# Where the mixer turns of a hybrid RG-LRU / attention block split three of their weight tiles

## The reference, cut to what matters

```python
xn = modulate(x, norm_mix_g, mx[0], mx[1]);  cn = modulate(ctx, norm_mix_g, mc[0], mc[1])
xr, kx, vx, gx, qx, mrx, mnx = jnp.split(xn @ w_in, IN_SPLITS, axis=-1)   # 7 column blocks of 1024
cr, kc, vc = jnp.split(cn @ w_in[:, :CTX_KV_COLS], [D_RNN, D_RNN + D_ATT], axis=-1)
h_x, _ = rglru_bidirectional(dwconv(xr), dwconv(cr), ...)                 # input branch
y_rnn = h_x * gelu(gx)
y_na = neighborhood_attention(rope_2d(qx), qx, rope_2d(kx), vx, kc, vc, na_rpb)
merged = sigmoid(mrx) * (y_rnn @ w_rnn_out) + sigmoid(mnx) * (y_na @ w_na_out)
x = x + mx[2] * (merged @ w_out)
x = x + mx[5] * conv_ffn(modulate(x, norm_ffn_g, mx[3], mx[4]), ...)
```

## Time and profile before

| | |
|---|---|
| median of three runs | 2131.47 us (2130.02 to 2133.41) |
| profiled execution, own time | 2128.76 us |
| its span | 2126.9 us |
| granted TensorE clock, mean | 0.997 of full speed |
| PE busy, share of the span | 2051.1 us, 96% |
| VectorE busy | 1628.0 us, 77% |
| ScalarE busy | 1072.5 us, 50% |
| GpSimd busy | 492.8 us, 23% |

### The profile page before, as it was taken

How to read it: one execution, slowest core, us unless ns; L and a number is a source line. 1 busy time by engine, 2 the same in 40 slices (tenths; PEclk the granted TensorE clock), 3 DMA queues, 4 the chain that set the end, 5 groups by cost and what they waited for, 6 DMA issues and landing times.

```text
span 2126.9 us, 28320 instructions
## 1 busy us (share of the span) xinstructions
PE 2051.1 (96%) x10618; PEld 1739.8 (82%) x10618; DVE 1628.0 (77%) x2809; ACT 1072.5 (50%) x1631; POOL 492.8 (23%) x377
## 2 busy tenths in 40 slices
PE   5999999999999999999998899999999999999999
PEld 1878888988988889888887788887788888887887
DVE  6688598596885985859859866767998888877766
ACT  3466666665676657656666621002444334434332
POOL 0031130222212212212123010000124442115550
PEclk9999999999999999999999999999999999999999
DMA  8421211112012120120111385453347764239663
GB/s 328 112 64 41 62 51 47 47 53 70 30 41 72 40 73 20 53 70 30 43 50 69 106 310 193 144 188 131 89 134 197 183 176 118 94 122 335 226 205 126
DMA packets 105576, 241.65 MB, mean 114 GB/s; under 512 B 27264, under 2 KB 32768, under 8 KB 104960
## 3 DMA queue, kind: packets, MB, share of 16 engines
q1 hardware_dynamic: 74304, 191.08, 26.4%
q0 software_dynamic: 14592, 44.05, 8.0%
q10 hardware_dynamic: 16544, 4.72, 1.0%
HBM read 203.11 MB, written 63.96 MB: 126 GB/s over the span
## 4 chain that ended last, share of the span: by engine, by line
PE 77%; DVE 13%; ACT 4%; issue 2%; ACTq 0%; DVEq 0%
PE banks L47 14%; PE banks L49 14%; PE banks L48 14%; PE banks L991 4%; PE banks L862 4%; PE banks L864 4%; PE banks L863 4%; PE banks L895 3%; PE banks L2269 3%; PE banks L2270 3%; PE banks L2271 3%; DVE probT_low L1494 2%; PE banks L953 2%; DVE prob L1486 2%; PE banks L935 1%
## 5 line engine op out<-in xcount | busy, mean ns | idle before, releaser
L47 PE MATMUL banks<-qh,xnh 128*128 128x384 f32 (+1 forms) x640 | 223.3, 349 | 0.3 <-PEq L216 0.3
L862 PE MATMUL banks<-xnh,wh 128*128 128x512 f32 (+1 forms) x536 | 211.3, 394 | 3.2 <-ACT stage L1097 2.9
L49 PE MATMUL banks<-qh,xnl 128*128 128x384 f32 (+1 forms) x640 | 207.7, 325 | 0.0
L48 PE MATMUL banks<-ql,xnh 128*128 128x384 f32 (+1 forms) x640 | 207.6, 324 | 0.0
L864 PE MATMUL banks<-xnh,wl 128*128 128x512 f32 (+1 forms) x536 | 204.5, 381 | 0.0
L863 PE MATMUL banks<-xnl,wh 128*128 128x512 f32 (+1 forms) x536 | 204.1, 381 | 0.0
L1494 DVE TENSOR_TENSOR probT_low<-banks,probT_high 128x512 fp32r<-128x512 f32 (+2 forms) x256 | 138.9, 583 | 56.2 <-ACT probT_high L1165 55.2
L1165 ACT CAST probT_high<-banks 128x512 fp32r<-128x512 f32 (+2 forms) x256 | 117.0, 510 | 60.3 <-PE banks L953 51.4
L47 PE MATMUL banks<-yh,wh 128*128 128x512 f32 x372 | 145.0, 390 | 0.9 <-DVE wl L2471 0.9
L48 PE MATMUL banks<-yl,wh 128*128 128x512 f32 x372 | 145.0, 390 | 0.0
L49 PE MATMUL banks<-yh,wl 128*128 128x512 f32 x372 | 144.9, 390 | 0.0
(11 more groups left out here) (396 smaller groups left out, 6015.9 us busy)
## 6 DMA issues: line engine op xcount, KB each, us to landing
raw<-w_ff SPq DMA_DIRECT2D x33, 512.0 KB, 5.7
down_d<-w_down POOLq DMA_DIRECT2D x66, 256.0 KB, 6.9
raw<-w_fm SPq DMA_DIRECT2D x32, 512.0 KB, 6.7
extras<-h_d SPq DMA_DIRECT2D x55, 256.0 KB, 3.9
raw<-w_qkv SPq DMA_DIRECT2D x24, 512.0 KB, 3.9
raw<-w_mix SPq DMA_DIRECT2D x24, 512.0 KB, 4.8
h_d<-conv_d SPq DMA_DIRECT2D x21, 512.0 KB, 3.2
raw<-w_modT SPq DMA_DIRECT2D x16, 512.0 KB, 4.6
```

The lines of the kernel that those rows point to most:

```text
L47: pe.matmul(out, w_hi(k), x_hi(k), start=(k == 0), stop=False)
L48: pe.matmul(out, w_hi(k), x_lo(k), start=False, stop=False)
L49: last = pe.matmul(out, w_lo(k), x_hi(k), start=False, stop=(k == chunks - 1))
L862: pe.matmul(out, fh[:, s, k, :], xnh[:, k, c0:c1], start=(k == 0), stop=False)
```

## The change

- Middle turns: `split_hi`/`split_low` of XR and MR go behind query tile 1 and its gates. 
- Turns 0 to 6: `split_hi(MN)` goes in front of `branch(F_MR)`, behind the last conv input (the input branch's last matmul); `split_low(MN)` goes in front of `maxima(0)`.
- Last turn: `split_hi(MN)`/`split_low(MN)` go behind query tile 1, so that MN is now split before MR; `LAST_ORDER` and one wait of SP follow. `split_hi(MR)`/`split_low(MR)` stay.
- Turn 0 keeps its splits of XR and MR where they were.

```diff
--- before.py
+++ after.py
@@ -587,7 +587,7 @@
         SLOT = {XR: 0, G: 1, MR: 1, MN: 0}
         RAW = {Q0: 0, Q1: 1, Q2: 2, XR: 0, MR: 1, MN: 2, G: 0}
         ORDER = {Q0: 0, Q1: 1, Q2: 2, XR: 3, MR: 4, MN: 5, G: 6}
-        LAST_ORDER = {Q0: 0, Q1: 1, Q2: 2, MR: 3, MN: 4}
+        LAST_ORDER = {Q0: 0, Q1: 1, Q2: 2, MN: 3, MR: 4}
 
         def split_count(u, i, last=False):
             return i * UNITS + 2 + (LAST_ORDER if last else ORDER)[u] + 1
@@ -747,7 +747,7 @@
                     store_stage(smr_d, i, 1, 1)
                     store_stage(smn_d, i, 0, 2)
                     sp.wait_ge(yr_out, PAIRS * 16)
-                    sp.wait_ge(w_lo, split_count(MN, i, True))
+                    sp.wait_ge(w_lo, split_count(MR, i, True))
                     for k in range(2):
                         load_y(k)
                     sp.dma_start(raw[:, 2, :], w_mix[0]).then_inc(mix_in, 16)
@@ -1222,6 +1222,8 @@
                     for s in range(1, 4):
                         q_evac(i, s)
                         gate_pieces(i, *GATES_LAST[s])
+                        if s == 1:
+                            split_hi(MN, raw_count(MN, i))
                     decays(i, 0)
                     q_evac(i, 4)
                     root(i, 0)
@@ -1233,6 +1235,9 @@
                     for s in range(3):
                         q_evac(i, s, first)
                         gate_pieces(i, *GATES_AFTER[s])
+                        if s == 1:
+                            split_hi(XR, raw_count(XR, i))
+                            split_hi(MR, raw_count(MR, i))
                     decays(i, 0)
                     q_evac(i, 3)
                     q_evac(i, 4)
@@ -1240,11 +1245,10 @@
                     gate_pieces(i, *GATES_AFTER[4])
                     q_evac(i, 5)
                     gate_pieces(i, *GATES_AFTER[5])
-                if not last:
+                if first:
                     split_hi(XR, raw_count(XR, i))
-                split_hi(MR, raw_count(MR, i))
-                if last:
-                    split_hi(MN, raw_count(MN, i))
+                if first or last:
+                    split_hi(MR, raw_count(MR, i))
                 q_evac(i, 6)
                 gate_pieces(i, *(GATES_FIRST if first else GATES_AFTER)[6])
                 if first:
@@ -1522,6 +1526,11 @@
                     outputs(i - 1, GROUPS_ATT - 1, False)
                 for s in range(4):
                     head_squares(i, s)
+                    if s == 1 and last:
+                        split_low(MN, i, True)
+                    elif s == 1 and not first:
+                        split_low(XR, i)
+                        split_low(MR, i)
                 if first:
                     dve.wait_ge(const_in, 32)
                     then(dve.tensor_scalar(gqk[:, 0, :], gqk[:, 0, :], HD ** -0.5, None, ALU.mult))
@@ -1537,9 +1546,10 @@
                 if not first:
                     head_squares(i, 5)
                     mean_squares(i, 0)
-                if not last:
+                if first:
                     split_low(XR, i)
                     split_low(MR, i)
+                if not last:
                     head_squares(i, 6)
                 inverse_roots(i, 0)
                 head_norm(1, *CHUNKS[0])
@@ -1547,7 +1557,6 @@
                     head_norm(0, NCT, CHUNKS[0][1])
                     split_low(MR, i, True)
                     head_squares(i, 6)
-                    split_low(MN, i, True)
                 if first:
                     head_squares(i, 7)
                 gated_input(i, 1)
@@ -1569,6 +1578,8 @@
                 inverse_roots(i, 1)
                 normalize_keys(i, 1)
                 normalize_queries(i, 1)
+                if not last:
+                    split_low(MN, i)
                 dve.wait_ge(bias_done, i * 3 + 3)
                 for u in range(2):
                     dve.wait_ge(qk_done, i * ATT + u + 1)
@@ -1576,8 +1587,6 @@
                     maxima(i, u)
                 v_low(i)
                 tr_low(i, JOBS_B)
-                if not last:
-                    split_low(MN, i)
                 for u in range(ATT):
                     probT_low(i, u)
                     inverse(i, u)
```

## The result

The changed kernel takes 2137.52 us (median of eight runs, 2134.95 to 2140.43) where the kernel before takes 2131.3 us (median of eight, 2130.02 to 2133.41). The ratio is 1.003 with a 95% interval of 1.0021 to 1.0038: slower by 6.2 us, between 4.5 and 8.1.

The account below looks back on a forecast made before the run. TensorE was taken as the bound, its one long middle-turn wait 1.3 us at `prob_transposes(1)`. MN's low part in turns 0 to 6 gave +3.4 to +4.5 us, +4.1 taken, other parts 0: 2135.6 us, range 2130.8 to 2138.0.

Parts of the forecast that it names:

- XR and MR: Early splits in turns 1 to 6: gain 0, cost 0, bounds -0.2 and +0.3 us a turn.
- the anchor of 409.83: Point in turn 2 until which VectorE waits for GpSimd's powers; work removed ahead of it was to become idle time.
- that of 416.43: Point in turn 2 where VectorE waits for ScalarE's square; at most its 0.20 us of waiting would grow.
- The weighed rule: At GpSimd's powers: by the rule the subtractions hold them up by 2.4 us; the forecast said the trace disagrees.
- Steps 1 to 4: Turn 2: L1489 held to 445.73, `soft(0)` 1.34 us later, qpS at 451.75, `prob_transposes(0)` at 451.9 after 0.7 us wait.
- Step 5: Turn 2: `prob_transposes(1)` released by ScalarE's `soft(1)`, 2.53 to 2.69 us after `prob_transposes(0)`; VectorE there by about 454.1.
- step 6: Turn 2: `prob_transposes(1)` at 454.43 to 454.59 instead of 453.96, +0.47 to +0.63 us a turn.
- Turn 0: MN's subtraction holds GpSimd's first stage operation, L1489 ends with the second, 1.45 us later; +0.6 to +0.7 us.
- The last turn: MN's cast and subtraction behind query tile 1 in turn 7: cost 0, bounds -0.1 and +0.5 us.
- the one that had the hold absent: Rival at `maxima(0)`: L1489 not held by GpSimd, 0 to +0.2 us a turn, 2132.2 us; chance 0.20.
- The one that misses GpSimd's gap: Rival: L1489 held to the end of GpSimd's second stage operation, 1.1 us more a turn, 2142.2 us; chance 0.10.
- The second rival: If `maxima(0)` is not late, the wait at `prob_transposes(1)` shrinks 0.2 us a turn, 2129.9 us, bound 2122.0; chance 0.08.

Follow-up runs that it names:

- e2_low_back: The whole change, but MN's subtraction put back behind `tr_low(i, JOBS_B)`, its cast still early; 2131.55 us, ratio 0.9998 to the kernel before.
- e3_pool_waits: The whole change, with GpSimd's first stage operation of the rnn gate waiting until the first minimum is done; 2132.02 us, ratio 1.0007 to the kernel before.
- e5_piece_first: The kernel before, with the first piece of the na gate's matmuls ahead of `prob_transposes(1)` instead of behind it; 2129.95 us, ratio 0.9991.
- e1_mn_only: The kernel before with only MN's cast and subtraction moved, in turns 0 to 6; 2137.32 us, ratio 1.0027.
- the first four experiments: The runs `e1_mn_only`, `e2_low_back`, `e3_pool_waits` and `e4_low_after_maxima`; the kernel before had a median of 2131.55 us beside them.
- e4_low_after_maxima: The whole change, with MN's subtraction behind both `maxima`, ahead of `v_low(i)`; 2136.27 us, ratio 1.0025 to the kernel before.
- e9_low_mid: `e5_piece_first` with MN's cast early and its subtraction between the low parts of qpS and qrS; 2132.98 us, ratio 1.0009 to the kernel before.

## Why the prediction was right and wrong

**What bounds the kernel.** Right: the changed kernel's longer turn is explained by the two waits in front of `prob_transposes(0)` and `(1)`. That turn 2 counts six times held too: the changed kernel falls back by another 3.94 us between the ends of turns 0 and 6.

**XR and MR.** Right, cost 0 (`e2_low_back`). The two casts end at 390.57, and ScalarE still idles 1.65 us before the next query tile, taken as 1.5; VectorE's cover is 0.93 us, taken as 0.9. The time freed ahead of the powers became idle time, as predicted: the anchor of 409.83 stands at 414.86 with the same idle time (0.43 us), that of 416.43 at 421.46 with the same 0.20, and VectorE idles 3.50 us before the squares at 414.02.

**The weighed rule.** By the Trainium skill, page "SBUF — State Buffer", section "Who interferes with whom", VectorE's operations with two SBUF inputs and GpSimd's that read SBUF exclude each other for the whole instruction. For GpSimd's stage and exchange operations the runs agree: 0.16 to 0.58 us for the minimum, 1.49 to 2.33 for `v_low`, 1.22 to 1.71 for the subtraction, and 0.16 again when GpSimd waits (`e3_pool_waits`). For the powers they don't: the subtractions beside them took 1.20 us each, and the power's own 4.17 us stayed 4.17 us when they were taken away.

**MN, step by step.** Steps 1 to 4 came as written. The minimum ends with GpSimd's operation (450.75 and 450.74, 445.73 predicted in the frame of before, 445.74 measured), `soft(0)` at 445.78 (445.77), `prob_transposes(0)` at 451.93 (451.9). Step 5 was half right: the wait is ended by ScalarE, 2.68 us after `prob_transposes(0)`. The upper end of 2.69 us was the true one. The lower end, 2.53 us, ran only to the end of `soft(1)`, and TensorE begins 0.05 us after that. The other 0.10 us are the gap between the two casts and the exponential, 0.88 us (458.54 against 457.66) where the kernel before has 0.73, less 0.05 us that the steps beside it lost; `e2_low_back` has the 0.88 us too. That VectorE would be there by 454.1 was also short: its half ended at 454.29, and with 0.15 us more it would have held TensorE to 454.44, just beyond the lower end by itself. So step 6 is 0.65 us a turn, above its range of 0.47 to 0.63, and six turns 3.9 us, where the sum had 2.8 to 3.8.

**Turn 0.** The size was short, and the mechanism partly another. Predicted was that the subtraction holds GpSimd's first operation and that L1489 is held to the end of the second. It was the other way round: GpSimd's first began ahead, at 164.76, and held the subtraction, and GpSimd's second then took 1.90 us; the minimum was not held (0.16 us). VectorE's, GpSimd's and TensorE's timelines of turn 0, to be read against the earlier trace rows with 3.49 us taken off:

```profile
165.03 2.06 DVE L1323 TENSOR_TENSOR wl<-raw,wh 128x1024 fp32r<-128x1024 f32 x1
```

```profile
164.76 1.25 POOL L803 TENSOR_TENSOR stage<-stage,one 128x512 f32<-128x512 f32 x1 [9.34 <-ACT stage L1097]
166.09 1.90 POOL L806 TENSOR_TENSOR stage<-stage,half_one 128x512 f32<-128x512 f32 x1
```

```profile
174.59 0.63 PE L953 MATMUL banks<-cst,prob 128*128 128x128 f32 x4 [2.85 <-DVE qpS L1457]
...
177.28 0.66 PE L953 MATMUL banks<-cst,prob 128*128 128x128 f32 x4 [1.15 <-ACT prob L1155]
```

`prob_transposes(0)` at 171.10 (predicted 170.96), `prob_transposes(1)` at 173.79 (173.5 to 173.65): +0.9 us where +0.6 to +0.7 stood. Who is first there is not the change's doing alone: in `e5_piece_first`, which leaves the subtraction in its place, GpSimd's first operation also comes 0.28 us after the start of VectorE's last rotation, where it came 1.34 us after it in the kernel before. And turn 0 repeats less well than the others: `e1_mn_only` has the same program in it and lost 1.4 us there (2.94, of which 1.54 before the subtraction). So +0.9 is the price in one execution.

**The last turn.** Cost 0 was predicted. It grew by 0.21 us; but with the last turn left alone (`e1_mn_only`) it grew by 0.33, and with it moved (`e2_low_back`) by 0.03. The granted clock of that turn was 1.00 before and in `e2_low_back`, 0.99 in the other two. So nothing of it need belong to the move. The subtraction was held here too, 1.75 instead of 1.22 us beside GpSimd's bias operation, ahead of nobody that mattered.

**The sum.** 3.9 + 0.9 = 4.8 us by the profile, against +4.1 taken and a range of 3.4 to 4.5. The medians say 6.2, with 4.8 inside their interval (4.5 to 8.1). The 1.4 us between them is not explained. The start of the mixer varies by more than that, and turn 0 by 0.5 us. The granted clock of the runs could hold some of it: beside the first four experiments the kernel before took 2129.0 us on average at 0.997 and 2132.2 at 0.994, and seven of the eight runs of the changed kernel had 0.994 or 0.995. Beyond that, the other kernels' medians miss the sum of their turns in both directions: `e4_low_after_maxima` lost 0.98 us in each of six turns, 5.9 us in them alone, and its median is only 4.7 us up.

**The step that failed.** The mechanism of the middle turns held; what was short is a term, the lower end of step 5, 2.53 us where 2.68 was measured, together with turn 0 (+0.6 to +0.7 where +0.9 was measured). With them went the choice of +4.1 us, where the turns give 4.8. It lay just under the 4.3 us that stood for 0.2%, so that 0.7 us decided the side. Of the rivals the one that had the hold absent is ruled out by the minimum's 0.58 us and `e3_pool_waits`. The one that misses GpSimd's gap is out as well: the minimum got in between the two operations in turn 2. The second rival's condition, that `maxima(0)` is not late, was not met: the minimum began 1.16 us later (445.16 against 444.00). Its price of 0.2 us a turn was never run; the ends of the chains put it at 0.21 us with the cast of MN in its old place and at 0.08 us with the cast early.

## What to carry to other kernels

Before work is moved ahead of a small step on a critical chain, look at what the other engines do at the new time: here 1.22 us of moved work cost 0.22 us by its length and 0.43 us because a minimum of 128 elements slid under a GpSimd operation. A wait of 1.3 us with one releaser named is not 1.3 us to be had, where a second engine's chain would end it 0.1 to 0.2 us earlier; read both chains to their ends before pricing a removal or a reordering, and then the chain of the step that follows. When two chains end within hundredths of a microsecond of each other, the name in the profile does not decide; the usual time from release to start does. A cost that is repeated per turn should be priced from a turn in which the neighbours wait as they will after the change.

## What the runs showed of the hardware

- GpSimd's operations on `stage`, the exchanges and the bias hold VectorE's operations with two SBUF inputs (1.49 to 2.33 us in `e4_low_after_maxima`, 1.22 to 1.71 in `e9_low_mid`, 1.22 to 1.75 in the changed kernel's last turn), and those on `stage` are held by them (1.04 to 2.12 us in `e4_low_after_maxima`). The powers on GpSimd, 4.17 us long, do neither. Why they differ no run here shows.
- At the head of the attention loop TensorE began 0.14 or 0.15 us after the end of the VectorE operation that it waited for, and 0.04 to 0.06 us after the end of ScalarE's exponential, in every kernel here.
- An exponential on ScalarE begins 0.72 or 0.73 us after the first pair of casts in the middle turns of the kernel before, and 0.88 or 0.89 us after it in those of `e2_low_back` and of the changed kernel. It does not go by waiting just before the casts: the next pair in the same turn has 0.76 us after 0.92 us of waiting (kernel before, casts at 454.62), and pairs later in the turn have 0.85 without any. The cause stays open.
- From one execution to the next the mixer's first load is issued up to 3 us apart (83.2 to 86.3 us), with no change in the code ahead of it; the later ones go with a granted clock of 0.92 instead of 0.96 up to there. The middle turns of one kernel repeat to 0.07 us.
